# Gate columns carried in the mLSTM value group and turned to rows; running maxima broadcast from fp32r parts

## The reference

```
ig = i_pre                                  # input gate,  6 columns of z, plus a bias
lf = log_sigmoid(f_pre)                     # forget gate, 6 columns of z, plus a bias
b  = cumsum(lf)                             # along the tokens, per head
a  = ig - b ;  A = running max of a         # per head
d(t, j) = exp(a_j - A_t) for j <= t         # weights of the scores
out = (q k^T / 8 * d) v / max(|den|, exp(-(b + A)))
```

## Time and profile before

| | us |
|---|---|
| median of three runs (lowest to highest) | 1569.66 (1569.42 to 1573.54) |
| span of the profiled execution | 1567.2 |
| TensorE busy in it | 1532.4 (98%) |
| VectorE, ScalarE, GpSimd busy | 824.6, 723.4, 317.8 |

### The profile page before, as it was taken

One profiled execution on the slowest core, in us unless ns is written; L12 is line 12 of the kernel. 1 busy time (PEld: TensorE's weight loads), 2 busy tenths in 40 slices (PEclk: granted clock), 3 DMA queues, 4 the chain that ended last, 5 costly groups with the idle time before them and its releaser, 6 DMA issues. The chain is left out here.

```text
span 1567.2 us, 22136 instructions
## 1 busy us (share of the span) xinstructions
PE 1532.4 (98%) x9018; PEld 1288.9 (82%) x9018; DVE 824.6 (53%) x1405; ACT 723.4 (46%) x1402; POOL 317.8 (20%) x270
## 2 busy tenths in 40 slices
PE   7999998999999999999999999999999999999999
PEld 6888887998898887888888888668887888888887
DVE  5346556556435755745234443668956544244442
ACT  4346545455654544544124443567844443134431
POOL 0000142001430001344013431032001433024420
PEclk9999999999999999999999999999999999999999
DMA  6212112323220103233223332110022333223331
GB/s 234 75 41 88 54 55 89 129 68 108 78 89 27 39 1 108 82 107 119 90 79 102 100 111 75 48 44 14 16 66 81 105 97 122 80 81 98 114 111 41
DMA packets 37462, 128.07 MB, mean 82 GB/s; under 512 B 4192, under 2 KB 8944, under 8 KB 37360
## 3 DMA queue, kind: packets, MB, share of 16 engines
q1 hardware_dynamic: 37360, 126.65, 24.9%
HBM read 124.54 MB, written 2.10 MB: 81 GB/s over the span
## 5 line engine op out<-in xcount | busy, mean ns | idle before, releaser
L321 PE MATMUL bank<-hhi,whi 128*128 128x512 f32 (+2 forms) x1064 | 418.3, 393 | 2.8 <-ACT hhi L1936 1.8
L323 PE MATMUL bank<-hhi,wlo 128*128 128x512 f32 (+2 forms) x1064 | 414.4, 390 | 0.0
L322 PE MATMUL bank<-hlo,whi 128*128 128x512 f32 (+2 forms) x1064 | 414.2, 389 | 0.0
L312 DVE TENSOR_TENSOR wlo<-wstage,whi 128x1024 fp32r<-128x1024 f32 (+9 forms) x250 | 278.6, 1117 | 112.2 <-ACT whi L302 111.8
L302 ACT CAST whi<-wstage 128x1024 fp32r<-128x1024 f32 (+9 forms) x250 | 236.1, 949 | 135.6 <-PE bank L323 131.7
L2421 DVE SCALAR_TENSOR_TENSOR cr<-bank,vc,cr 128x511 f32<-128x511 f32 (+1 forms) x168 | 125.9, 749 | 217.1 <-ACT cr L2360 214.1
L321 PEld LDWEIGHTS bank<-hhi,whi 128*128 128x128 f32 (+2 forms) x1064 | 198.7, 187 | 49.3 <-ACT hhi L1936 4.3
L323 PEld LDWEIGHTS bank<-hhi,wlo 128*128 128x128 f32 (+2 forms) x1064 | 198.6, 187 | 43.2
L322 PEld LDWEIGHTS bank<-hlo,whi 128*128 128x128 f32 (+2 forms) x1064 | 198.7, 187 | 41.7 <-issue 0.5
L2360 ACT ACTIVATE cr<-bank,vc 128x512 f32<-128x512 f32 x84 | 65.5, 780 | 248.5 <-PE bank L323 246.1
L2466 POOL TENSOR_TENSOR cr<-cr,cr 128x512 f32<-128x512 f32 x44 | 94.4, 2146 | 315.4 <-DVE cr L2421 280.7
(11 more groups left out here) (412 smaller groups left out, 2298.5 us busy)
## 6 DMA issues: line engine op xcount, KB each, us to landing
wstage<-in_wts SPq DMA_DIRECT2D x147, 512.0 KB, 3.5
wstage<-in_wts SPq DMA_DIRECT2D x32, 704.0 KB, 4.0
wstage<-in_wts SPq DMA_DIRECT2D x14, 768.0 KB, 4.3
xT<-in_x SPq DMA_DIRECT2D x4, 512.0 KB, 5.3
xt<-in_x SPq DMA_DIRECT2D x4, 512.0 KB, 5.9
out<-ob SPq DMA_DIRECT2D x8, 256.0 KB, 2.3
U<-in_rel_ext SPq DMA_DIRECT2D x6, 256.0 KB, 9.0
wstage<-in_wts SPq DMA_DIRECT2D x2, 603.0 KB, 3.9
```

The source lines that it names most:

```text
L312: e.tensor_tensor(K.wlo[i % 3][:, p], K.stage[i % 3][:, p], K.whi[i % 3][:, p].bitcast(F32), SUB).then_inc(*K.dve.up(("wlo", i) if last el ...
L321: e.matmul(o, lh, rh, start=start, stop=False)
L322: e.matmul(o, lh, rl, start=False, stop=False)
L323: return e.matmul(o, ll, rh, start=False, stop=stop)
```

## The change

The 12 gate columns and the 16 `ga` columns become columns 384 to 411 of the mLSTM value group `mv`. Its weights come as three chunks of 3, 3 and 2 row blocks with 412 columns (widths 1236, 1236, 824), where there were two of 1536 and one of 384. The `mv` group moves ahead of `mqk0` and runs in pairs of token tiles: both banks of the ring are taken at the start of a pair, and the parts are gone through for both tiles. The slots after:

```
+    for two in ((0, 1), (2, 3)):
+        for c in two:
+            K.RP.take(q, ("mv", 0, "c", c))
+        for n, (part, c) in enumerate((p, c) for p in range(3) for c in two):
+            if c == two[0]:
+                i, hi, lo = parts[part] = parts.get(part) or K.chunk(q, "mv", 0, part)
+            b = K.bank(("mv", 0, "c", c))
+            for k in range(3 * part, min(8, 3 * part + 3)):
+                z = mm3(e, b[:, 0:412], x.hi[:, k, c * P:(c + 1) * P], ...)
+            if n in (2, 5):
+                yield
...
+    fm(("mqk", 1))
+    b = K.RO1.take(q, "gateT")
+    for c in range(4):
+        z = e.transpose(b[0:80, c * P:(c + 1) * P], K.gtok[:, c, :], K.ident[:])
...
 VectorE, step 17:
+    dve_log_sigmoid(e, q, K, "fr", K.fr, 6)
+    e.tensor_tensor_scan(K.Fsum, ones6, K.fr, 0.0, MUL, ADD)...
+    e.tensor_tensor(K.aj[0:6, :], K.gts[0:6, :], K.Fsum, SUB)...
+    e.tensor_tensor_scan(K.Am, ...)...
+    e.tensor_tensor(K.em, K.Fsum, K.Am, ADD)...
     conv(1)
     conv_silu(3)
...
 ScalarE, step 17:
     conv(1)
     conv_silu(3)
+    e.activation(K.gts[:], K.bank("gateT")[0:80, :], ACT.Identity, bias=K.bg[:, 0:1])...
+    act_log_sigmoid(e, q, K, "fr", K.fr, 6)
...
 pe_ml:
-                e.matmul(b[:], K.ident[64:70, 64 + h:65 + h].to_broadcast([6, P]), K.Am, ...)
+                e.matmul(b[:], K.sela[:, h:h + 1].to_broadcast([64, P]), K.amr[:], ...)
```

More of the change, by code:

```diff
@@ L59, in plan_chunks @@
     tm("av", "w_in", 0, 768, 384)
-    out["gate", 0] = ("gates", None, 0, 8, 0, 48)
+    for part, (k0, kt) in enumerate(FV_K):
+        out["mv", 0, part] = ("values", None, k0 * P, kt, 0, 412)
     tm("mo", "w_in", 0, 2688, 384)
@@ L603, in pe_den @@
     yield from pe_tiles(e, q, K, "av", 0, x, 4, 384)
[L604 to L614, removed]
+    for key in (("ak", 1), ("aq", 2), ("ak", 2)):
+        fm(key)
+        yield
+    parts = {}
+    for two in ((0, 1), (2, 3)):
[6 more added lines that the diff above has]
+            for k in range(3 * part, min(8, 3 * part + 3)):
+                q.wait_ge(*K.at((x.gen, "lo", k)))
+                z = mm3(e, b[:, 0:412], x.hi[:, k, c * P:(c + 1) * P], x.lo[:, k, c * P:(c + 1) * P],
+                        hi[:, k - 3 * part, :], lo[:, k - 3 * part, :], k == 0, k == 7)
+            z.then_inc(*K.pe.up(("mv", 0, part, "c", c), *([("mv", 0, "c", c)] if part == 2 else []), *([K.used(i)] if c == 3 else [])))
+            if n in (2, 5):
+                yield
     fm(("mqk", 0))
     yield
[L618 to L624, removed]
     fm(("mqk", 3))
@@ L627, in pe_den @@
     fm(("mqk", 1))
-    b = K.RO1.take(q, "ajT")
-    q.wait_ge(*K.at("aj"))
+    b = K.RO1.take(q, "gateT")
     for c in range(4):
[L631 to L635, removed]
+        q.wait_ge(*K.at(("gtok", c)))
+        z = e.transpose(b[0:80, c * P:(c + 1) * P], K.gtok[:, c, :], K.ident[:])
+    z.then_inc(*K.pe.up("gateT"))
     yield
@@ L638, in pe_den, with rows @@
     yield
-    yield from pe_tiles(e, q, K, "mo", 0, x, 4, 384)
+    def rows(c):
+        if c == 1:
+            b = K.RO1.take(q, "ajT")
+            q.wait_ge(*K.at("aj"))
+            for i in range(4):
+                e.transpose(b[:, i * 6:i * 6 + 6], K.aj[0:6, i * P:(i + 1) * P], K.ident[0:6, 0:6])
+            q.wait_ge(*K.at("em"))
+            for i in range(4):
+                z = e.transpose(b[:, 24 + i * 6:30 + i * 6], K.em[:, i * P:(i + 1) * P], K.ident[0:6, 0:6])
+            z.then_inc(*K.pe.up("ajT"))
+        if c == 2:
+            b = K.RO1.take(q, "alrow")
+            e.matmul(b[:], K.wal[64:80, :], K.gts[64:80, :], start=True, stop=True).then_inc(*K.pe.up("alrow"))
+    yield from pe_tiles(e, q, K, "mo", 0, x, 4, 384, rows)
     for i in (2, 5):
@@ L697, in act_den @@
     yield
[L698 to L703, removed]
     aqk(2)
@@ L706, in act_den @@
     akk(2)
-    q.wait_ge(*K.at("frow"))
-    e.copy(K.fr, K.bank("frow")[0:6, :]).then_inc(*K.act.up(("fr", "pre"), frees=["frow"]))
-    act_log_sigmoid(e, q, K, "fr", K.fr, 6)
     yield
+    for c in range(4):
+        if c % 2 == 1:
+            c -= 1
+            b = ("mv", 0, "c", c)
+            q.wait_ge(*K.at("gtok0"))
+            q.wait_ge(*K.at("mva1"))
+            q.wait_ge(*K.at(b))
+            for n, (o, i) in enumerate(gate_columns(K, c)):
+                e.copy(o, i).then_inc(*K.act.up(("gtok", c) if n else ("gtok", c, 0)))
+            act_evac(e, q, K, ("mva", c), b, K.mva[:, c, :, 0:64],
+                     K.bank(b)[:, 0:384].rearrange("p (h n) -> p h n", h=6))
+        yield
     conv(0)
     yield
[L713 to L727, removed]
     conv(3)
-    act_log_sigmoid(e, q, K, "al", K.tmp["al"][:], P)
+    conv_silu(0)
     yield
@@ L732, in act_den @@
     conv_silu(3)
+    q.wait_ge(*K.at("gains1"))
+    q.wait_ge(*K.at("gateT"))
+    e.activation(K.gts[:], K.bank("gateT")[0:80, :], ACT.Identity, bias=K.bg[:, 0:1]).then_inc(
+        *K.act.up("gts", ("fr", "pre"), frees=["gateT"]))
+    act_log_sigmoid(e, q, K, "fr", K.fr, 6)
     yield
@@ L744, in act_den @@
             conv_silu(4)
+        if c == 2:
+            t = K.tmp.take(q, "al")
+            q.wait_ge(*K.at("alrow"))
+            e.activation(t[:], K.bank("alrow")[:], ACT.Identity, bias=K.col("b_alpha")).then_inc(
+                *K.act.up(("al", "pre"), frees=["alrow"]))
+            act_log_sigmoid(e, q, K, "al", K.tmp["al"][:], P)
         yield
@@ L811, in dve_den @@
     yield
-    yield
     aqk(2)
@@ L816, in dve_den @@
     yield
+    for c in range(4):
+        if c % 2 == 1:
+            b = ("mv", 0, "c", c)
+            q.wait_ge(*K.at("gtok0"))
+            q.wait_ge(*K.at("mva1"))
+            q.wait_ge(*K.at(b))
+            for n, (o, i) in enumerate(gate_columns(K, c)):
+                e.tensor_copy(o, i).then_inc(*K.dve.up(("gtok", c) if n else ("gtok", c, 0)))
+            dve_evac(e, q, K, ("mva", c), b, K.mva[:, c, :, 0:64],
+                     K.bank(b)[:, 0:384].rearrange("p (h n) -> p h n", h=6))
+        yield
@@ L817, in dve_den @@
     conv(0)
     yield
[L819 to L838, removed]
@@ L855, in dve_den @@
     conv_silu(1)
+    q.wait_ge(*K.at("amr0"))
+    e.tensor_copy(K.amr[0:6, :], K.Am).then_inc(*K.dve.up("amh"))
+    q.wait_ge(*K.at("amh"))
+    e.tensor_tensor(K.amr[32:38, :], K.Am, K.amr[0:6, :].bitcast(F32), SUB).then_inc(*K.dve.up("amr"))
+    e.tensor_tensor(K.sela[:], K.ident[0:64, 0:6], K.ident[0:64, 32:38], ADD).then_inc(*K.dve.up("sela"))
     yield
@@ L859, in dve_den @@
             conv_silu(4)
+        if c == 1:
+            q.wait_ge(*K.at("ajT"))
+            e.tensor_copy(K.acol[:].rearrange("p a b -> p (a b)"), K.bank("ajT")[:, 0:24]).then_inc(*K.dve.up("acol"))
+            e.tensor_copy(K.ecol[:].rearrange("p a b -> p (a b)"), K.bank("ajT")[:, 24:48]).then_inc(
+                *K.dve.up("ecol", frees=["ajT"]))
+        if c == 3:
+            al = K.tmp["al"][:]
+            dve_log_sigmoid(e, q, K, "al", al, P)
+            e.tensor_scalar(al, al, 1.0 / 16.0, None, MUL).then_inc(*K.dve.up("al16"))
+            q.wait_ge(*K.at("al16"))
+            e.tensor_tensor_scan(K.bT[:], K.ones[:, 0:1].to_broadcast([P, T]), al, 0.0, MUL, ADD).then_inc(
+                *K.dve.up("bT", frees=["al"]))
         yield
@@ L908, in pool_den @@
     e.memset(K.mva[:, :, :, 64:65], 1.0).then_inc(*K.pool.up("mva1"))
-    yield from steps(26)
+    for c in range(4):
+        q.wait_ge(*K.at(("yt", c)))
+    q.wait_ge(*K.pool.last())
+    e.memset(K.amr[:].bitcast(F32), 0.0).then_inc(*K.pool.up("amr0"))
+    yield from steps(25)
     for c in range(4):
@@ L1281, in pe_ml @@
         if u < 12 and u % 4 == 0:
-            q.wait_ge(*K.at("Am"))
+            q.wait_ge(*K.at("amr"))
+            q.wait_ge(*K.at("sela"))
             for h, J in ml_pair(u):
                 b = K.RT1.take(q, ("ml", "A", h))
-                e.matmul(b[:], K.ident[64:70, 64 + h:65 + h].to_broadcast([6, P]), K.Am, start=True, stop=True).then_inc(
+                e.matmul(b[:], K.sela[:, h:h + 1].to_broadcast([64, P]), K.amr[:], start=True, stop=True).then_inc(
                     *K.pe.up(("ml", "A", h)))
@@ L2894, in schedule @@
     out = ["init"] + ["x"] * 2 + ["den"] * 4 + ["den", "att", "att"] * 17
-    ml = weave(("ml", 18), ("den", 14))
+    ml = weave(("ml", 18), ("den", 13))
     for i in range(5):
@@ L2946, in pieces @@
         n = SCHEDULE[0:g].count(name)
[L2947 to L2948 removed]
+        out.append(1 if name in QUARTERS or name == "gla" or name == "lat" and n >= 4 or name == "den" and 38 <= n <= 41 else 0)
+        if name == "gla" and n == 4 or name == "den" and n == 37:
             out[g] = 2
@@ L3105, in memory @@
     K.tmpd = Ring(K, [Buffer(K, b.t) for b in K.tmp.buffers[3:5]])
+    with ExitStack() as s:
+        K.amr = sb("amr", [64, T], F32R, s)
     K.hold = ring("hold", 1, [P, T])
@@ L3275, in lay_out @@
     a = {k: np.asarray(v) for k, v in inputs.items()}
```

(4 more changed lines are left out.)

39 lines of the change are left out of this document (28 added, 11 removed).

## The result

| | before | after |
|---|---|---|
| median of 5 interleaved runs, us | 1570.13 (1569.42 to 1573.54) | 1578.81 (1578.17 to 1579.77) |
| ratio after/before | | 1.0049 [1.0033, 1.0064] |
| span of the profiled execution, us | 1567.2 | 1577.5 |

The change makes the kernel 0.5% slower: 8.7 us in the medians, 10.3 between the two profiled spans. I had forecast 1575.2 within 1563 to 1580, slower with a chance of 0.50. The sign and the mechanism hold. The size was 3.6 us short: the median lies within the range, but 0.8 above the narrower 1572 to 1578 that I gave for the forecast alone.

A forecast was written before the change was run, and what follows sets the result against it. TensorE, busy 98% of the span, was taken as the bound. -9.2 of its work, +13.2 of waits and +1.5 of clock gave +5.5 on 1567.2, so 1572.7; with the 2.5 offset 1575.2 us, range 1563 to 1580.

The forecast's parts named there:

- TensorE's own balance: TensorE's work: gate slot, broadcasts and forget-row selection saved, wider `mv` and transposes added; -9.2 us, bounds -7.3 and -9.8.
- term: 4.35: Six broadcasts as single fp32r products instead of fp32: 4.35 us saved on TensorE, bounds 3 to 4.4.
- The four waits: TensorE waits for ring banks at slots 10, 12, 14, 18: 2.75, 2.3, 1.9, 6.9 us; net +13.2, bounds 7 and 18.
- the 0.61 of before: Before's wait of `mo 0` for a convolution to free its bank, 0.61 us, forecast to go.
- The clock, +1.5 once: One fall of TensorE's granted clock behind the wait of slot 18: +1.5 us, bounds 0 and 3.
- The offset of the runs, 2.5: Median of the runs stands 2.5 us above the profiled span; kept, taking 1572.7 to 1575.2.
- forecast 165: Start of the first broadcast of `ml`, 150.74 before: near 165 us after.
- weave term: Order of `ml` steps in the weave with one `den` less: counted as 0 us, bounds -0.5 and +1.
- A: Waits don't arise or hide, ScalarE and VectorE finishing sooner; only -9.2 shows, 1560.5 us; chance 15%.
- B: The three `mv` waits come, but `conv(1)` is in time for slot 18; -2.8 us, 1567; chance 17%.
- C: The waits come without the fall of the clock; +4.0 us, 1573.7; chance 23%.
- D: Step 17's lateness runs on into slots 19, 20 and first `ml` steps; +4 to +5 more, 1580; chance 10%.

The follow-up runs named there:

- e4: Kernel before with only the six broadcasts made as fp32r products from parts: 1565.65 us, ratio 0.9957 to before.
- e7: e3 with the scan of the maxima and the sum for `em` moved behind `conv(4)`: 1559.36 us, ratio 0.9915 to before.
- e1: After, with `conv(1)` and `conv_silu(3)` moved ahead of the log-sigmoid chain in VectorE's step 17: 1572.47 us, ratio 1.0005 to before.
- e2: After, with `mv` made tile by tile, one bank at a time, and ScalarE copying tiles 0 and 2 one step earlier: 1571.42 us, ratio 0.9996 to before.
- e6: After, with `mv` still in pairs but the second bank taken only at its first product: 1573.12 us, ratio 1.0013 to before.
- e5: After, with unread extra matmuls, 10 ahead of slot 10 and 28 ahead of slot 18: 1581.95 us, ratio 1.0071 to before.
- e9: After once more, unedited, for a second profile: 1579.93 us, ratio 1.0047 to before.
- e3: After with the edits of e1 and e2, and `mqk0`'s weights split as soon as a chunk is free: 1561.7 us, ratio 0.9936 to before.

## Why the prediction was right, and where it was short

**TensorE's own balance, -9.2: right.** e4 gives 4.8 for the broadcasts alone (term: 4.35; by the rows of a pair 3 x 1.46 = 4.4), and e7, without any new wait up to 180 us, has the rest in rows: 5.5 up to the first broadcast, where 5.45 was due. Its span is 10.0 below before, with the wait of 1.18 for `hm` against it and the gap of 1.69 of before (both below) for it. The bounds that I gave for the sum, -7.3 and -9.8, are not what the bounds of its terms add up to, -6.8 and -9.7; nothing hung on them.

**The four waits: right in place, releaser and size.** Forecast 2.75, 2.3, 1.9 and 6.9; measured 2.64, 2.20, 1.68 and 6.92. With the 0.61 of before taken off they add 12.8 (forecast 13.2). They could be had from the trace of before since VectorE and ScalarE run their programs in order: e1 moves two calls and the 6.9 go, e2 changes what is taken and the first two go.

**The clock, +1.5 once: the step that failed in size.** I put a fall behind slot 18 alone and left the other three waits without one, and no row of mine gave a reason for that. The profile of after shows one behind each of the four waits. Against the same slots at the full clock (7.83 and 7.26 in e1, 8.21 in e6, 6.18 in e5), each from its first product to the next slot's, slots 10, 12, 14 and 18 took 9.38, 8.82, 9.82 and 8.29: 1.55 + 1.56 + 1.61 + 2.11 = 6.8 us. The Trainium skill, "TensorE: Matmul & The Clock Gate", Part 1, ties the fall to TensorE having stood idle. The trace agrees for the wait of 6.92 us (window at 0.50), and shows falls behind waits of 1.68 to 2.64 us as well.

**The offset of the runs, 2.5: should have been about 1.7.** Every run of after has its time 1.7 above its own span. That took 0.8 back. Another 0.4 is that the profiled execution of after lies that much above its median (1579.18 against 1578.81).

Together: -9.2 + 12.8 + 6.8 = +10.4, and the spans differ by 10.3. The close fit is in part luck, as what follows the first layer isn't nothing. Up to the first broadcast after is 19.96 us later (170.70 against 150.74), of which 4.3 is the moved `mo` tile. I had forecast 165; the missing 5 to 6 us are the falls of the clock. From there on to the end after gains 9.7 us: the moved tile, 4.35 for the broadcasts, and about 2 more less a new wait of 1.2 for `hm` at 238.5 us. The weave term that I set at 0 thus has a piece of +1.2, just past my bound of +1: every variant of after has this wait (1.18 to 1.22), and e4, which has the new broadcasts in the old weave, doesn't. About 2 us against it coincide with a gap of 1.69 us ("issue") at 250.17 in before which after doesn't have. Why that gap comes and goes I can't say; e5's are the same kind.

**Rivals.** A (the waits hide) and B (`conv(1)` in time) are refuted by the four rows. B failed as I argued, that step 17 can't begin before round 16: with 2.32 us of waits ahead of it (e2) instead of 6.52, slot 18 waited for the same 6.92. C (no fall) is refuted: each of the four windows of after shows one, and e9 three of four. D (step 17's lateness runs on) doesn't occur in after, where the slot behind `mo 0` takes its usual 5.9 us. It does occur in e1, where the long wait is gone: one cover hid the other.

## What to carry to other kernels

When work moves to an engine that isn't the bound, look for what is queued behind it on that engine, and for the buffer that the bound engine wants from there. Take a bank of a short ring when its first write is due, not with its neighbour: e6 shows this at the price of one moved call. Split a chain of small operations so that what frees a buffer goes between its parts (e7: the last wait of 1.90 is gone; with the edits of e3 the change goes from 0.5% slower to 0.9% faster), and charge a wait of 2 us in a full matmul stretch with its own length and a possible fall of the clock of nearly the same size.

## What the runs showed of the hardware

- Over the traces of after and its variants, with before's one wait: behind waits of 6.9 us a lower clock followed 4 times of 4; behind those of 1.7 to 2.7 us 13 times of 18; behind those up to 1.0 us never in 6. Each fall cost 1.6 to 2.8 us. Between 1.0 and 1.7 us there is no wait in these stretches, and why 5 of the 18 had no fall is open.
- The time of a run goes with its mean granted clock. The 29 runs of before on the chip of e1 go from 1566.07 us at 0.999 to 1579.98 at 0.991, about 1.3 us for each 0.001. So the clock also falls, by more in some executions than in others, in the kernel that has one wait of 0.61 us in these stretches; the profiled execution had 0.998, and where the others lost it no trace shows. The varying falls behind the waits are thus not needed to explain the range of e1 (1569.4 to 1575.2). A difference of two spans from one profile each carries this variation with it.
- A matmul of 412 columns followed the last after 0.187 us at the full clock and 0.34 at the lower level. Slot 10 with its wait of 2.64 us was in one state in after and in the other in e1.
- Gaps of 1.7 to 2.4 us named "issue" in the GLA stretch (250 to 295 us) come and go between kernels whose code there is the same. They limit what a difference of 2 us in span can show.
